# Attention stage: windowed heads taken in pairs with one maximum, and the turning of probabilities three steps behind the scores

## What is computed

```python
def _diff_core(q, k, v, lam):                      # group A, 4 heads, two maps of head size 32
    s = einsum('bqhmd,bkhmd->bhmqk', q, k) * 32 ** -0.5
    p = softmax(s, axis=-1)
    a = p[:, :, 0] - lam * p[:, :, 1]
    return einsum('bhqk,bkhe->bqhe', a, v)

def _sink_softmax(logits, sink):                   # group C, 4 query heads on 2 key/value heads, size 64
    m = maximum(max(logits, axis=-1, keepdims=True), sink)
    e = exp(logits - m)
    return e / (sum(e, axis=-1, keepdims=True) + exp(sink - m))
# latent queries: 256 context keys and a window of +-128 latent keys, the rest masked
```

## Time and profile before

| | us |
|---|---|
| median of 3 runs (1771.97 to 1772.33) | 1772.24 |
| the profiled execution | 1774.29 |
| its span, first to last instruction | 1772.4 |
| TensorE busy (share of the span) | 1704.0 (96%) |
| VectorE busy | 1224.6 (69%) |
| ScalarE busy | 377.2 (21%) |
| GpSimd busy | 236.2 (13%) |
| granted TensorE clock, mean | 0.997 |

### The profile page before, as it was taken

The page is one execution under the profiler, slowest core; times in us unless marked ns, Lnnn a source line. Parts: engine busy times, 40 slices in busy tenths (PEclk is TensorE's granted clock), DMA queues, the critical chain, the costliest instruction groups (busy, mean ns, idle before and its releaser), DMA issues.

```text
span 1772.4 us, 34791 instructions
## 1 busy us (share of the span) xinstructions
PE 1704.0 (96%) x15369; PEld 1084.0 (61%) x15369; DVE 1224.6 (69%) x1286; ACT 377.2 (21%) x695; POOL 236.2 (13%) x108
## 2 busy tenths in 40 slices
PE   6999999899999999999999888999999999999999
PEld 2334557674544444445465555968787787869695
DVE  1443476975444344115576877999999999999998
ACT  1101254453422222112125342010100000001100
POOL 0035100020656430000460010000000000000000
PEclk9999999999999999999999999999999999999999
DMA  9932201014656425231230126999999999999994
GB/s 375 329 143 72 95 1 48 1 49 152 229 193 235 181 104 190 71 95 48 96 119 1 48 106 259 407 410 419 412 419 413 418 407 419 414 415 414 411 416 189
DMA packets 98846, 408.77 MB, mean 231 GB/s; under 512 B 14009, under 2 KB 20857, under 8 KB 84369
## 3 DMA queue, kind: packets, MB, share of 16 engines
q1 hardware_dynamic: 96504, 405.54, 58.3%
q10 hardware_dynamic: 2200, 1.08, 0.2%
HBM read 405.55 MB, written 1.05 MB: 229 GB/s over the span
## 4 chain that ended last, share of the span: by engine, by line
PE 76%; DVE 8%; PEld 5%; issue 4%; DMA 3%; ACT 2%; PEldq 0%; ACTq 0%; SPq 0%; POOL 0%; DVEq 0%; POOLq 0%
PE PS L1669 12%; PE PS L803 10%; PE PS L2044 9%; PE PS L1627 6%; PE PS L2018 5%; PE PS L2020 5%; PE PS L2021 5%; PE PS L807 5%; PE PS L1533 2%; PE PS L485 2%; DMA ARENA<-in_moe_w 2%; PE PS L1395 2%; DVE ARENA L2140 2%; PEld PS L2044 2%; DVE ARENA L1008 1%
## 5 line engine op out<-in xcount | busy, mean ns | idle before, releaser
L2140 DVE TENSOR_TENSOR ARENA<-ARENA 128x2816 bf16<-128x2816 f32 (+2 forms) x184 | 567.0, 3121 | 23.7 <-DMA ARENA<-in_moe_w 22.6
L2018 PE MATMUL PS<-ARENA 128*128 128x96 bf16 x2816 | 379.1, 209 | 4.9 <-issue 1.9
L2020 PE MATMUL PS<-ARENA 128*128 128x96 bf16 x2816 | 378.9, 209 | 1.7 <-issue 1.5
L2021 PE MATMUL PS<-ARENA 128*128 128x96 bf16 x2816 | 378.8, 206 | 1.3 <-issue 1.0
L2020 PEld LDWEIGHTS PS<-ARENA 128*128 128x128 bf16 x2816 | 354.8, 126 | 9.6 <-issue 9.5
L2018 PEld LDWEIGHTS PS<-ARENA 128*128 128x128 bf16 x2816 | 346.3, 123 | 11.6 <-issue 9.5
L2021 PEld LDWEIGHTS PS<-ARENA 128*128 128x128 bf16 x2816 | 298.6, 106 | 2.1 <-issue 2.1
L803 PE MATMUL PS<-ARENA 128*128 128x512 bf16 (+1 forms) x1104 | 227.9, 356 | 0.0
L2044 PE MATMUL PS<-ARENA 128*96 128x512 bf16 x960 | 216.1, 384 | 0.2 <-DVE ARENA L2140 0.2
L1669 PE MATMUL PS<-ARENA 128*128 128x512 bf16 x984 | 215.8, 379 | 0.0
L2044 PEld LDWEIGHTS PS<-ARENA 128*96 128x96 bf16 x960 | 116.2, 122 | 93.1 <-issue 0.3
(11 more groups left out here) (252 smaller groups left out, 1820.2 us busy)
## 6 DMA issues: line engine op xcount, KB each, us to landing
ARENA<-in_moe_w SPq DMA_DIRECT2D x128, 1408.0 KB, 13.3
ARENA<-in_moe_w SPq DMA_DIRECT2D x48, 1536.0 KB, 16.0
ARENA<-in_ada_w SPq DMA_DIRECT2D x24, 2048.0 KB, 10.2
ARENA<-in_ffn_w SPq DMA_DIRECT2D x15, 2048.0 KB, 7.9
ARENA<-in_w_in SPq DMA_DIRECT2D x11, 2048.0 KB, 8.1
ARENA<-in_moe_w SPq DMA_DIRECT2D x16, 1024.0 KB, 15.8
ARENA<-in_w_in SPq DMA_DIRECT2D x6, 1024.0 KB, 8.7
ARENA<-in_w_out SPq DMA_DIRECT2D x8, 512.0 KB, 4.3
```

The source lines that it names most:

```text
L2018: pe.matmul(out, hi[:, h][:, f], HEH[:, k, :], start=k == 0 and b % 4 == 0, stop=False, skip_group_check=True)
L2020: pe.matmul(out, hi[:, h][:, f], HEL[:, k, :], start=False, stop=False, skip_group_check=True)
L2021: mm = pe.matmul(out, lo[:, h][:, f], HEH[:, k, :], start=False, stop=k == KC - 1, skip_group_check=True)
L2140: dve.tensor_tensor(WLO[q % NSLOT][:, 0:n], RAW[q % NSLOT][:, 0:n], WHI[q % NSLOT][:, 0:n], ALU.subtract).then_inc(S("m_lo"), 1)
```

## The change

Windowed heads h and h + 2 of a tile, which use the two halves of the array's rows, become one unit with two parts. Its two score products go into the unit's two banks, followed (latent) by two mask products; one maximum is taken over both banks; two scalings give two biases; ScalarE does sink, exponential, sink, exponential; the sums and reciprocals of both parts are taken together, and the copy of the reciprocal is gone. The units of a tile now come as D, W pair, D, D, W pair, D: six units with eight parts. Steps go by parts; at the second part of a pair no unit begins. Transposes, copies, values and output scalings still go part by part, now three steps behind the scores instead of two (`TURN_LAG`), values four, output five. There is one step more in a stage. Filler steps are spread over the new number of steps. The semaphore counts follow.

The diff, cut to its new side where a whole function changes (lines without a sign are unchanged, "..." marks what is left out; the old side stands in the functions above):

```diff
         def units(L):
-            return [(kind, h, x) for x in tiles(L) for h in range(NH) for kind in "DW"]
+            return [("D", (h,), x) if kind == "D" else ("W", (h, h + 2), x)
+                    for x in tiles(L) for kind, h in (("D", 0), ("W", 0), ("D", 1), ("D", 2), ("W", 1), ("D", 3))]
+
+        def parts_of_units(L):
+
+            return [(u, m, kind, h, x) for u, (kind, hs, x) in enumerate(units(L)) for m, h in enumerate(hs)]
+
+        def unit_begun(L, s):
+
+            ps = parts_of_units(L)
+            return ps[s][0] if s < len(ps) and ps[s][1] == 0 else None
+
+        TURN_LAG = 3
 
         def keys(x):
...
-            total, steps = KC * (att_units(L) - 1), len(units(L)) + 3
+            total, steps = KC * (att_units(L) - 1), len(parts_of_units(L)) + TURN_LAG + 1
...
         def pe_att(pe, L):
...
+            for s in range(len(ps) + TURN_LAG + 1):
+                u = unit_begun(L, s)
+                if u is not None:
+                    kind, hs, x = us[u]
+                    if u >= 2:
+                        pe.wait_ge(S(n + "exp"), since(L, n + "exp") + u - 1)
                     c, nk = slice(P * x, P * x + P), keys(x)
+                    for m in range(2):
+                        bank = B(2 * (u % 2) + m)
+                        if kind == "D":
+                            g = 2 * hs[0] + m
+                            r = slice(32 * (g % 4), 32 * (g % 4) + 32)
+                            mm = pe.matmul(bank[:, 0:nk], QKT[r, g // 4, c], QKT[r, 2 + g // 4, 0:nk], start=True, stop=True)
+                        else:
+                            r = slice(64 * (hs[m] // 2), 64 * (hs[m] // 2) + 64)
+                            mm = pe.matmul(bank[:, 0:nk], CT[r, hs[m] % 2, c], CT[r, 2, 0:nk], start=True, stop=True)
+                    if kind == "W" and x in LAT_TILES:
+                        o = 384 if x == 2 else 256
                         for m in range(2):
+                            mm = pe.matmul(B(2 * (u % 2) + m)[:, o:o + P], ident, kc(K_SWA)[:, P * (x - 2):P * (x - 1)],
                                            start=False, stop=True, skip_group_check=True)
                     mm.then_inc(S(n + "s"), 1)
                 for step in fill_range(L, s):
                     pe_proj_fill(pe, L, step)
+                if TURN_LAG <= s < len(ps) + TURN_LAG:
+                    v = s - TURN_LAG
+                    u, m, kind, h, x = ps[v]
+                    pe.wait_ge(S(n + "p"), since(L, n + "p") + v + 1)
+                    if v >= 1:
+                        pe.wait_ge(S(n + "at"), since(L, n + "at") + v)
+                    for k in range(keys(x) // P):
+                        mm = pe.transpose(B(4)[:, P * k:P * k + P], EX[:, u % 4, m, P * k:P * k + P], ident)
                     mm.then_inc(S(n + "pt"), 1)
+                if s > TURN_LAG:
+                    v = s - TURN_LAG - 1
+                    u, m, kind, h, x = ps[v]
+                    pe.wait_ge(S(n + "at"), since(L, n + "at") + v + 1)
+                    if v >= 1:
+                        pe.wait_ge(S(n + "o"), since(L, n + "o") + v)
                     nk = keys(x) // P
                     for k in range(nk):
+                        values = AV[:, k, 64 * h:64 * h + 64] if kind == "D" else \
+                            CQKV[:, k, 384 + 64 * (h // 2):448 + 64 * (h // 2)]
+                        mm = pe.matmul(B(5)[:, 0:64], AT[:, v % 2, P * k:P * k + P], values, start=k == 0, stop=k == nk - 1)
                     mm.then_inc(S(n + "pv"), 1)
 
         def act_att(act, L):
+            n, us, ps = "a_", units(L), parts_of_units(L)
+            last_part = {part[0]: v for v, part in enumerate(ps)}
             act_proj_one(act, L, FIRST)
+            for s in range(len(ps) + TURN_LAG + 1):
+                u = unit_begun(L, s)
+                if u is not None:
+                    kind, hs, x = us[u]
                     nk = keys(x)
+                    act.wait_ge(S(n + "nb"), since(L, n + "nb") + u + 1)
+                    if u >= 4:
+                        act.wait_ge(S(n + "pt"), since(L, n + "pt") + last_part[u - 4] + 1)
+                    for m in range(2):
+                        if kind == "W":
+                            act.activation(AST[:, 3, u, m:m + 1], SINK[:, L, hs[m]:hs[m] + 1], ACT.Exp,
+                                           bias=AST[:, 1, u, m:m + 1])
+                        ins = act.activation(EX[:, u % 4, m, 0:nk], B(2 * (u % 2) + m)[:, 0:nk], ACT.Exp,
+                                             bias=AST[:, 1, u, m:m + 1], scale=32 ** -0.5 if kind == "D" else 64 ** -0.5,
+                                             accum_out=AST[:, 2, u, m:m + 1])
                     ins.then_inc(S(n + "exp"), 1)
                 for step in fill_range(L, s - 1) if s else ():
                     if step % KC == KC - 1:
                         act_proj_one(act, L, FIRST + step // KC)
+                if TURN_LAG <= s < len(ps) + TURN_LAG:
+                    v = s - TURN_LAG
+                    nk = keys(ps[v][-1])
+                    act.wait_ge(S(n + "pt"), since(L, n + "pt") + v + 1)
+                    if v >= 2:
+                        act.wait_ge(S(n + "pv"), since(L, n + "pv") + v - 1)
+                    act.activation(AT[:, v % 2, 0:nk], B(4)[:, 0:nk], ACT.Copy).then_inc(S(n + "at"), 1)
             act_proj_one(act, L, FIRST + att_units(L) - 1)
 
         def dve_att(dve, L):
+            n, us, ps = "a_", units(L), parts_of_units(L)
+            differences = 0
+            for s in range(len(ps) + TURN_LAG + 2):
+                if s >= TURN_LAG + 2:
+                    v = s - TURN_LAG - 2
+                    u, m, kind, h, x = ps[v]
+                    dve.wait_ge(S(n + "pv"), since(L, n + "pv") + v + 1)
                     c = (0 if kind == "D" else 256) + 64 * h
+                    dve.tensor_scalar(MIXAC[:, x, c:c + 64], B(5)[:, 0:64], AST[:, 4, u, m:m + 1], None,
                                       ALU.mult).then_inc(S(n + "o"), 1)
+                u = unit_begun(L, s)
+                if u is not None:
+                    kind, hs, x = us[u]
+                    dve.wait_ge(S(n + "s"), since(L, n + "s") + u + 1)
+                    dve.tensor_reduce(AST[:, 0, u, :], PS[:, 2 * (u % 2):2 * (u % 2) + 2, 0:keys(x)], AX.X,
+                                      ALU.max).then_inc(S(n + "mx"), 1)
+                    dve.wait_ge(S(n + "mx"), since(L, n + "mx") + u + 1)
                     if kind == "D":
+                        ins = dve.tensor_scalar(AST[:, 1, u, :], AST[:, 0, u, :], -(32 ** -0.5), None, ALU.mult)
                     else:
+                        for m, h in enumerate(hs):
+                            ins = dve.tensor_scalar(AST[:, 1, u, m:m + 1], AST[:, 0, u, m:m + 1], -(64 ** -0.5),
+                                                    NSINK[:, L, h:h + 1], ALU.mult, ALU.min)
+                    ins.then_inc(S(n + "nb"), 1)
+                u = unit_begun(L, s - 1) if s else None
+                if u is not None:
+                    kind, hs, x = us[u]
                     nk = keys(x)
                     dve.wait_ge(S(n + "exp"), since(L, n + "exp") + u + 1)
                     if kind == "D":
+                        differences += 1
                         dve.reciprocal(AST[:, 4, u, :], AST[:, 2, u, :]).then_inc(S(n + "r"), 1)
+                        dve.wait_ge(S(n + "r"), since(L, n + "r") + differences)
 
                         dve.tensor_scalar(AST[:, 5, u, 0:1], AST[:, 4, u, 1:2], AST[:, 2, u, 0:1], LAM[:, L, 5:6],
                                           ALU.mult, ALU.mult).then_inc(S(n + "ratio"), 1)
                         dve.scalar_tensor_tensor(out=e, in0=EX[:, u % 4, 1, 0:nk], scalar=AST[:, 5, u, 0:1], in1=e,
                                                  op0=ALU.mult, op1=ALU.add).then_inc(S(n + "p"), 1)
                     else:
+                        dve.tensor_tensor(AST[:, 5, u, :], AST[:, 2, u, :], AST[:, 3, u, :], ALU.add).then_inc(S(n + "ratio"), 1)
                         dve.wait_ge(S(n + "ratio"), since(L, n + "ratio") + u + 1)
+                        dve.reciprocal(AST[:, 4, u, :], AST[:, 5, u, :]).then_inc(S(n + "p"), 2)
```

More of the change, by code:

```diff
@@ L247, in trunk @@
                 in_layer0.update({f"h{d}{p}_upd": 1 + 3 * len(LEVELS)})
-        for step in ("s", "mx", "nb", "exp", "r", "ratio", "p", "pt", "at", "pv", "o"):
+        for step in ("p", "pt", "at", "pv", "o"):
             in_layer0["a_" + step] = 2 * NH * NT
+        for step in ("s", "mx", "nb", "exp", "ratio"):
+            in_layer0["a_" + step] = 6 * NT
+        in_layer0["a_r"] = NH * NT
         def since(L, name):
@@ L1349, in pe_att @@
         def pe_att(pe, L):
-            n, us = "a_", units(L)
+            n, us, ps = "a_", units(L), parts_of_units(L)
             for step in range(KC):
@@ L1377, in pe_att @@
                     pe_proj_fill(pe, L, step)
[L1378 to L1384, removed]
```

(30 more changed lines are left out.)

55 lines of the change are left out of this document (removed).

## The result

The changed kernel takes 1804.57 us (median of 4 runs, 1803.58 to 1813.08) against 1772.28: 1.0188 times the time of before, 95% interval 1.017 to 1.0206, or 32.3 us slower. 1781.3 was forecast. The direction was right; the size was short by 23 us.

The account below looks back on a forecast made before the run. TensorE's work and the chain over the copy were both taken to bound the 6.11 us latent period. Longer pair chains add 3.4 us (layer 1) and 5.7 (layer 0): 1772.24 + 9.1 = 1781.3 us, range 1778 to 1786.

Parts of the forecast that it names:

- What bounds the kernel: Attention stages: TensorE's work list and the chain over the copy of AT both fill the 6.11 us latent period.
- (1) W scores in pairs: TensorE: products on distinct row groups overlap, saving 1.05 us per latent pair, about 0.6 in a context tile.
- (3): Second mask product ahead of a latent pair's maximum: +0.33 us, could be 0.52 or about 0.2.
- (4): ScalarE's second sink and exponential before the copy: +0.86 us latent, +0.65 context; TensorE waits about 2.2 us.
- the pair's chain: Latent pair: 5.27 us from scores to copy, 6.01 to the next transposes, 7.41 for the two steps.
- (5) the double D: Two D units in a row: the first's chain holds the second's transposes; 6.11 us latent, 3.85 context.
- The walk: Step-by-step sum of the stages: layer 1 59.7 against 56.30 us, layer 0 92.1 against 86.45; together +9.1.
- The sign that hung on the same step: New profile: TensorE's busy time in the stages falls while they grow to about 92 and 60 us.
- the slow end of the range, 1789: Upper end of the 8-in-10 range, half the way to the serial-products rival (1792 us, chance 0.08).
- (6): Turning three steps behind: adds a step per stage; the copy wait stays one step deep, so no chain gain.
- The faster rival: Attention stages: TensorE is the bound if the copy is ready within its own work; -14 us, 1758; chance 0.08.

Follow-up runs that it names:

- a_busy: Changed kernel with never-read stand-in matrix products where TensorE would wait for the copy of AT, at each pair's second step; ratio 1.0063, 1785.54 us.
- a_cf_o_lag2: a_cf_o with TURN_LAG = 2, so transposes two steps behind the scores; ratio 1.0058.
- a_cf_o: Changed kernel with the copy of AT ahead of the exponentials and VectorE's output scaling between maximum and sums; ratio 0.9892, 1756.78 us.
- b_more3: Kernel before, single heads, with three more never-read exponentials per W unit ahead of the copy; 1847.22 us in a single run.

## Why the prediction was wrong, point by point

- **What bounds the kernel** held. The two bounds of a latent period met at 6.11 us as read, and the shift of a stage passed on whole: what lies behind moved by 0.3 and 0.4 us.
- **(1) W scores in pairs** held in kind. Two products take 1.13 us; the packing is worth 0.85 us a latent pair, not 1.05, and 0.43 a context pair, not 0.6.
- **(3), (4), the pair's chain**: 5.88 us measured for 6.01, two steps in 7.28 for 7.41. The two mask products held TensorE for 0.55 us (262.37 to 262.92) where one had held it for 0.33, so the second took 0.2 and not the 0.33 that I chose; the lower bound was right.
- **(5) the double D**: in a_busy 6.12 us (scores at 264.75 to scores at 270.87) for 6.11.
- **The walk** for layer 1 gave 59.7; with the clock held by stand-ins it is 60.13. For layer 0 it gave 92.1 and a_busy has 95.54. Of these 3.4 us, 1.0 is a term that was too small: the second pair's scores come 9.83 us into the stage, in a_busy as in the changed kernel, and not 8.8, and no fall stands before them in either. Part of the rest is the one fall of the clock that is left (0.98 over the stage), behind the first double D unit, where no stand-ins stood and the copy was waited for 1.48 us.
- **The step that failed** is the one in (4) that says of TensorE "It waits about 2.2 us", and all sums that used it: a wait was priced at its own length. The prediction had the length right (2.15 measured) and had no term for what TensorE does after it. That term is at least 19 us, twice the whole forecast loss; the chain in the walk was too small by at most 3.8 us, and the two make the 22.8 us by which the stages grew more than the 9.1 that were summed. The sign that hung on the same step, TensorE's busy time falling while the stages grow, failed too: it rose from 82.09 to 92.92 us in layer 0. The section "What bounds the kernel" had looked at busy shares and at the chain, and the granted clock, 1.00 in both stages, was taken as given although the change was about to put gaps of 2 us into them. No rival had it either: the slow end of the range, 1789, came from products in series.
- **(6) "the lag does not help the chain"** held for the change as it is. What I added later, for a_cf_o_lag2, that the third step can be dropped once the copy is moved, did not: the difference of the maps then comes late, and 15.2 us of waits return (9.7 in layer 0, 5.5 in layer 1 of a_cf_o_lag2).
- **The faster rival** (1758, TensorE the bound) is about where the kernel lands when the two orders are mended: 1756.78. Its condition, the copy ready within TensorE's own work, was the right one. That the two numbers are 1 us apart is in part luck: on that chip a_cf_o is 18.7 us below before (17.2 in the stages), where the rival had summed 14, and with the copy alone moved TensorE still waited for the output scaling, for which the rival had no term.

## What to carry to other kernels

When a change adds a wait to an engine that was full, price what the engine does after the wait as well: look at TensorE's granted clock in that stretch, and if it is at its full level only because nothing waits there, put a fall into the sum or among the rivals. Before packing work on one engine, walk the in-order queue of the engine that drains it, and ask which short instruction that others wait for stands behind the work that the packing doubles; here moving one copy ahead of the exponentials turned a loss of 1.9% into a gain of 0.3%, and a second move made it 1%.

## What the runs showed of the hardware that was not expected

- Waits of 0.9 to 2.2 us between stretches of dense work were followed by falls of the clock from 2.4 to 1.2 GHz, though not all: single ones of 1.46, 1.51 and 1.91 us were not. At the places shown it falls after the wait, not in it: the transposes started at 267.19 at full clock, and the fall came near 269.4, in the midst of work. Nor does work always bring it back soon: 30 us of it in b_more3 did not.
- At 1.2 GHz the same records take 2.08 us for 1.13 (D scores) and 1.81 for 1.00 (values), so the chain, which runs over scores, transposes and values, gets longer too: these stages, bound by their chain, did not hide the fall.
- Filling a wait with 21 products that nobody reads (2.46 us at one place of a_busy, fewer at others) made the kernel 19 us faster, with nothing taken off the chain.
- Two f32 products of 64 rows and 512 columns on different rows: 1.06 us to the next work; on the same rows 1.91.
